# Last 32 tokens routed by pairs of heads, first v loads spread out, and constant inputs of VectorE held in PSUM

## The reference

```python
def block(xt):                                    # peer(): xt are normalised tokens
    qh = (xt @ w_pq).reshape(PEER_BLOCK, PEER_HEADS, 2, half)          # 8 heads x 2 halves
    sub = jnp.einsum('thcd,ckd->thck', qh, sub_keys)                   # 128 scores per half
    top_s, top_i = lax.top_k(sub, PEER_TOPK)                           # 16 best of 128
    cand = (top_s[:, :, 0, :, None] + top_s[:, :, 1, None, :]).reshape(PEER_BLOCK, PEER_HEADS, 256)
    best_s, best_c = lax.top_k(cand, PEER_TOPK)                        # 16 best of 256
    i1 = jnp.take_along_axis(top_i[:, :, 0], best_c // PEER_TOPK, axis=-1)
    i2 = jnp.take_along_axis(top_i[:, :, 1], best_c % PEER_TOPK, axis=-1)
    experts = i1 * PEER_KEYS + i2                                      # one of 128 x 128
    gate = jax.nn.softmax(best_s, axis=-1)
    pre = jnp.einsum('td,thkd->thk', xt, expert_u[experts])
    act = jax.nn.gelu(pre, approximate=False)
    return jnp.einsum('thk,thkd->td', gate * act, expert_v[experts])
```

## Time and profile before

| | us |
|---|---|
| three runs before | 2404.65, 2404.66, 2394.77 (median 2404.65) |
| the profiled execution | 2399.41, span 2397.4 |
| PE busy | 2081.4 (87%) |
| DVE busy | 1669.2 (70%) |
| POOL busy | 1186.3 (49%) |
| ACT busy | 776.1 (32%) |

### The profile page before, as it was taken

The page is one execution under the profiler, slowest core; times in us unless marked ns, Lnnn a source line. Parts: engine busy times, 40 slices in busy tenths (PEclk is TensorE's granted clock), DMA queues, the critical chain, the costliest instruction groups (busy, mean ns, idle before and its releaser), DMA issues.

```text
span 2397.4 us, 34751 instructions
## 1 busy us (share of the span) xinstructions
PE 2081.4 (87%) x12685; PEld 1930.0 (81%) x12685; DVE 1669.2 (70%) x3238; ACT 776.1 (32%) x1230; POOL 1186.3 (49%) x632
## 2 busy tenths in 40 slices
PE   5999998677569898998885888886979999999998
PEld 5989657565449898897784878786879999999998
DVE  2478434443322207699999999994549999999996
ACT  3233233321322324444342333332223333333332
POOL 2326003111003234675674343436888888888884
PEclk9999659895989899999997999998999999999999
DMA  6443255453853114566675666669869989988994
GB/s 223 149 154 112 100 200 216 191 185 103 283 187 132 53 36 154 187 228 208 193 233 173 208 229 244 238 231 336 289 227 324 320 306 318 315 315 308 320 322 143
DMA packets 176598, 520.95 MB, mean 217 GB/s; under 512 B 15153, under 2 KB 86065, under 8 KB 170705
## 3 DMA queue, kind: packets, MB, share of 16 engines
q1 hardware_dynamic: 136560, 290.94, 35.3%
q0 software_dynamic: 36864, 134.23, 17.0%
q10 hardware_dynamic: 3056, 94.24, 9.9%
HBM read 456.81 MB, written 128.49 MB: 244 GB/s over the span
## 4 chain that ended last, share of the span: by engine, by line
DVE 44%; PE 36%; issue 7%; POOL 5%; DMA 3%; ACT 3%; SPq 2%; ACTq 0%; DVEq 0%; PEldq 0%
DVE acc_g L1809 9%; DVE act_l L1793 9%; PE bank L2169 8%; PE bank L2170 7%; PE bank L2171 7%; DVE one L1493 6%; DVE one L1494 5%; DVE rows_g L1662 4%; POOL u_lo L1637 3%; DMA ks<-kc 2%; POOL rows_g L1652 2%; PE bank L438 2%; PE bank L457 1%; DVE eq L1470 1%; PE bank L639 1%
## 5 line engine op out<-in xcount | busy, mean ns | idle before, releaser
L1637 POOL TENSOR_TENSOR u_lo<-u_raw,u_hi 128x1024 fp32r<-128x1024 f32 x128 | 327.8, 2562 | 328.7 <-ACT u_hi L1617 327.7
L2169 PE MATMUL bank<-hn_hi,u_hi 128*128 128x416 f32 x1024 | 381.2, 372 | 67.5 <-POOL u_lo L1637 67.2
L1837 POOL TENSOR_TENSOR v_lo<-v_raw,v_hi 128x1024 fp32r<-128x1024 f32 x128 | 335.4, 2622 | 68.5 <-ACT v_hi L1762 67.3
L2170 PE MATMUL bank<-hn_lo,u_hi 128*128 128x416 f32 x1024 | 368.7, 360 | 0.0
L2171 PE MATMUL bank<-hn_hi,u_lo 128*128 128x416 f32 x1024 | 366.8, 358 | 0.0
L2169 PE MATMUL bank<-a_hi,v_hi 128*128 128x416 f32 x1024 | 360.7, 352 | 1.8 <-DVE a_lo L1799 1.7
L2170 PE MATMUL bank<-a_lo,v_hi 128*128 128x416 f32 x1024 | 358.9, 350 | 0.0
L2171 PE MATMUL bank<-a_hi,v_lo 128*128 128x416 f32 x1024 | 358.8, 350 | 0.0
L1809 DVE SCALAR_TENSOR_TENSOR acc_g<-rows_g,coef,acc_g 128x1024 f32<-128x1024 f32 x127 | 289.2, 2277 | 13.8 <-DMA rows_g<-ev,idx_g 13.3
L2169 PEld LDWEIGHTS bank<-hn_hi,u_hi 128*128 128x128 f32 x1024 | 200.0, 195 | 86.7 <-POOL u_lo L1637 84.1
L1662 DVE CUSTOM_DVE_ANT_0 rows_g<-rows_g,xrep 128x1024 f32<-128x1024 f32 x128 | 187.2, 1466 | 83.0 <-DMA rows_g<-eu_rows,idx_g 82.4
(11 more groups left out here) (360 smaller groups left out, 4358.4 us busy)
## 6 DMA issues: line engine op xcount, KB each, us to landing
u_raw<-eu SPq DMA_DIRECT2D x128, 512.0 KB
v_raw<-ev SPq DMA_DIRECT2D x128, 512.0 KB
k_s<-kc ACTq DMA_DIRECT2D x29, 1104.0 KB
v_s<-vc ACTq DMA_DIRECT2D x29, 1104.0 KB
acts_dram<-act_c SPq DMA_DIRECT2D x128, 208.0 KB
gates_dram<-gst ACTq DMA_DIRECT2D x8, 3328.0 KB, 12.8
gin<-gates_dram SPq DMA_DIRECT2D x32, 832.0 KB
act_l<-acts_dram SPq DMA_DIRECT2D x64, 416.0 KB
```

What stands on the lines that cost most here:

```text
L1637: nc.gpsimd.tensor_tensor(out=u_lo[s][:], in0=u_raw[2 * (x % 2) + s][:], in1=u_hi[s][:].bitcast(F32), op=ALU.subtract).then_inc(dn["ulo"], 1)
L1837: nc.gpsimd.tensor_tensor(out=v_lo[f % 4][:], in0=v_raw[f % 4][:], in1=v_hi[f % 4][:].bitcast(F32), op=ALU.subtract).then_inc(dn["vlo"], 1)
L2169: nc.tensor.matmul(out, ah, bh, start=first and i == 0, stop=False)
L2170: nc.tensor.matmul(out, ah, bl, start=False, stop=False)
```

## The change

Three things. First, part t = 4 (32 tokens) is laid out as four groups of 32 partitions, each with two of the eight heads (`HG` = 4): TensorE writes the scores of head pair g to partitions 32g to 32g + 31, one evacuation replaces four, and every routing step of DVE works on 128 partitions and a quarter of the elements. The turning becomes 12 small matmuls. Second, `load_first` is called at every step of x = 57 to 63 and issues one load at each of its first seven, in place of all eight after x = 50. Third, ACT copies `asc` to PSUM bank 7 and `xrep` to banks 2 and 3 (`twin`) once; DVE's one-hot tiles, the first compare of the lookup and the dots read them there.

```diff
+HG = P // ROUTE[-1][1]
+        x_held, asc_p = twin[:], bank[7][:, 0:P]
@@ sp_ffn
-                if x == LAST_X0:
-                    load_first(sp)
+                    load_first(sp, 2 * (x - FIRST_V + 3) + s)
@@ pe_ffn, half_scores(t)
+                if t == NT - 1:
+                    pe.wait_ge(ff["sub_evac"], 4 * t - 1)
+                    for j in range(4):
+                        for g in range(HG):
+                            last = nc.tensor.matmul(quad(4)[g * w:(g + 1) * w, j, :], qt[:, 4 * g + j, t0:t0 + w], skt_s[:, j % 2, :],
+                                                    start=True, stop=True)
+                    last.then_inc(ff["sub"], 1)
+                    return
@@ pe_ffn, turn_picks(t)
+                if t == NT - 1:
+                    for j in range(3):
+                        for g in range(HG):
+                            last = nc.tensor.matmul(bank[6][g * w:(g + 1) * w, j * P:j * P + w], picks[:, j, 0:PICKS // HG],
+                                                    ident[:, g * w:(g + 1) * w], start=True, stop=True)
@@ act_ffn
             split_u(act, 0, 0, 0)
+            nc.scalar.activation(asc_p, asc, ACT.Copy).then_inc(sx["held"], 1)
+            few_wait(act, "x_in", 32)
+            for b in range(2):
+                nc.scalar.activation(x_held[0:NG, 512 * b:512 * (b + 1)], xrep[0:NG, 512 * b:512 * (b + 1)], ACT.Copy).then_inc(sx["held"], 1)
@@ dve_ffn
-            few_wait(dve, "x_in", 32)
+            few_wait(dve, "held", 3)
             for t, (t0, w) in enumerate(ROUTE):
-                dve.wait_ge(ff["sub_evac"], 4 * (t + 1))
-                top16(t, w, lambda j: tv[0:w, j, :], lambda j: ti[0:w, j, :], lambda j: sub_t[0:w, j, :], 2 * PH)
+                heads = PH
+                if t < NT - 1:
+                    dve.wait_ge(ff["sub_evac"], 4 * (t + 1))
+                else:
+                    dve.wait_ge(ff["sub_evac"], 4 * t + 1)
+                    w, heads = P, PH // HG
+                top16(t, w, lambda j: tv[0:w, j, :], lambda j: ti[0:w, j, :], lambda j: sub_t[0:w, j, :], 2 * heads)
...
-                                  in1=bc(asc[0:w, 0:TOPK], 1, PH * TOPK), op=ALU.is_equal))
-                    chain.link(tt(out=eq[0:w], in0=eq[0:w], in1=bc(tif4[:, :, c, :], 2, TOPK), op=ALU.mult))
+                                  in1=bc(asc_p[0:w, 0:TOPK], 1, heads * TOPK), op=ALU.is_equal))
+                    chain.link(tt(out=eq[0:w, 0:heads], in0=eq[0:w, 0:heads], in1=bc(tif4[:, :, c, :], 2, TOPK), op=ALU.mult))
...
-                    ts(one2[n % HOT][:, j, :], asc, picks_t[:, 1, c:c + 1], None, ALU.is_equal)
-                    last = ts(one1[n % HOT][:, j, :], asc, picks_t[:, 0, c:c + 1], picks_t[:, 2, c:c + 1], ALU.is_equal, ALU.mult)
+                    ts(one2[n % HOT][:, j, :], asc_p, picks_t[:, 1, c:c + 1], None, ALU.is_equal)
+                    last = ts(one1[n % HOT][:, j, :], asc_p, picks_t[:, 0, c:c + 1], picks_t[:, 2, c:c + 1], ALU.is_equal, ALU.mult)
@@ dots
-                nc.vector.tensor_tensor_reduce(out=row, in0=row, in1=xrep[0:NG, :], scale=1.0, scalar=0.0, op0=ALU.mult, op1=ALU.add,
+                nc.vector.tensor_tensor_reduce(out=row, in0=row, in1=x_held[0:NG, :], scale=1.0, scalar=0.0, op0=ALU.mult, op1=ALU.add,
@@ load_first(sp, step)
+            if step == 0:
+                for b in range(2):
+                    sp.wait_ge(gate_out[b], 16 * (GBLOCKS // 2) + 16)
+                load_gates(sp, 0, 0)
+            elif step in (1, 6):
+                load_acts(sp, step // 6, step // 6)
+            elif step in (2, 3):
+                load_v(sp, step - 2, step - 2)
+            elif step == 4:
...
+            elif step == 5:
+                load_gates(sp, 1, 1)
```

More of the change, by code:

```diff
@@ L60 @@
 ROUTE = [(DT, NG)] + [(t0, min(P, DT - t0)) for t0 in range(0, DT, P)]
+HG = P // ROUTE[-1][1]
+assert HG == 4
 ROW_SLOTS, MORE_SLOTS = 3, 5
@@ L1330, in scores_out @@
                     act.wait_ge(ff["sub_free"], t - 1)
+                if t == NT - 1:
+                    act.wait_ge(ff["sub"], 4 * t + 1)
+                    nc.scalar.activation(sub_s[t % 2][:, 0:4, :], quad(4), ACT.Copy).then_inc(ff["sub_evac"], 1)
+                    return
                 for g in range(4):
@@ L1344, in act_ffn @@
                 act.wait_ge(ff["top_exp"], t + 1)
-                nc.scalar.activation(bv[0:w], bv[0:w], ACT.Exp).then_inc(ff["top_expd"], 1)
+                w, heads = (w, PH) if t < NT - 1 else (P, PH // HG)
+                nc.scalar.activation(bv[0:w, 0:heads], bv[0:w, 0:heads], ACT.Exp).then_inc(ff["top_expd"], 1)
             act.sem_inc(ff["gate_bank"], 2)
-            few_wait(act, "x_in", 32)
             with act.Fori(0, GBLOCKS // GB) as i:
@@ L1466, in dve_ffn @@
                 for c in range(2):
-                    chain.link(tt(out=eq3, in0=bc(bhlf[0:w, c].rearrange("p h k -> p (h k)"), 2, TOPK),
-                                  in1=bc(asc[0:w, 0:TOPK], 1, PH * TOPK), op=ALU.is_equal))
-                    chain.link(tt(out=eq[0:w], in0=eq[0:w], in1=bc(tif4[:, :, c, :], 2, TOPK), op=ALU.mult))
+                    chain.link(tt(out=eq3, in0=bc(bhlf[0:w, c, 0:heads].rearrange("p h k -> p (h k)"), 2, TOPK),
+                                  in1=bc(asc_p[0:w, 0:TOPK], 1, heads * TOPK), op=ALU.is_equal))
+                    chain.link(tt(out=eq[0:w, 0:heads], in0=eq[0:w, 0:heads], in1=bc(tif4[:, :, c, :], 2, TOPK), op=ALU.mult))
                     dots(dve, t, 1)
-                    chain.link(nc.vector.tensor_reduce(picks[0:w, c, :], eq3, axis=AX.X, op=ALU.add))
+                    chain.link(nc.vector.tensor_reduce(picks[0:w, c, 0:heads * TOPK], eq3, axis=AX.X, op=ALU.add))
                 dots(dve, t, 1)
                 dve.wait_ge(ff["top_expd"], t + 1)
-                chain.link(nc.vector.tensor_reduce(gsum[0:w, 0, :], bv[0:w], axis=AX.X, op=ALU.add))
-                chain.link(nc.vector.reciprocal(gsum[0:w, 1, :], gsum[0:w, 0, :]))
-                weights = gate_w if t == 0 else picks[:, 2, :]
-                last = tt(out=weights[0:w].rearrange("p (h k) -> p h k", k=TOPK), in0=bv[0:w], in1=bc(gsum[0:w, 1, :], 2, TOPK), op=ALU.mult)
+                chain.link(nc.vector.tensor_reduce(gsum[0:w, 0, 0:heads], bv[0:w, 0:heads], axis=AX.X, op=ALU.add))
+                chain.link(nc.vector.reciprocal(gsum[0:w, 1, 0:heads], gsum[0:w, 0, 0:heads]))
+                weights = gate_w if t == 0 else picks[:, 2, 0:heads * TOPK]
+                last = tt(out=weights[0:w].rearrange("p (h k) -> p h k", k=TOPK), in0=bv[0:w, 0:heads], in1=bc(gsum[0:w, 1, 0:heads], 2, TOPK),
+                          op=ALU.mult)
                 if t:
@@ L1672, in load_gates, with load_first @@
             sp.dma_start(gin[s][:], gates_dram[:, :, bass.ds(4 * k, 4), :].rearrange("b p a t -> p b (a t)")).then_inc(g_in[s], 16)
[L1674 to L1684 removed]
+        def load_first(sp, step):
+            if step == 0:
[7 more added lines that the diff above has]
+            elif step == 4:
+                head = NG - NB * NL
+                sp.dma_start(xg[0:head, :], X[P - head:P, NT - 2, :]).then_inc(sx["xg_in"], 16)
+                sp.dma_start(xg[head:NG, :], X[0:NB * NL, NT - 1, :]).then_inc(sx["xg_in"], 16)
+            elif step == 5:
+                load_gates(sp, 1, 1)
         def sp_dense(sp):
```

44 lines of the change are left out of this document (20 added, 24 removed).

## The result

The changed kernel takes 2326.71 us (median of four runs, 2321.80 to 2331.31), the kernel before in the same comparison 2404.65 (2394.77 to 2409.90). The ratio is 0.968, 95% interval 0.9643 to 0.9717. Run again later it took 2324.92 (five runs), 0.9662 (0.9647 to 0.9677). The profiled execution took 2327.75, its span is 2325.8, its granted clock 0.938 of 2.4 GHz.

The account below looks back on a forecast made before the run. DVE was taken to bound the gate stage and parts t = 2 and 4, PE the dense stage. 2399.4 - 31 (routing) - 18 (gates) - 18 (tail) = 2332, plus 2 gives 2334 us; range about 2312 to 2362.

Parts of the forecast that it names:

- first loads' contention: Tail: first loads meet busy DMA engines, so stores and u tiles come late; 3 us counted against the gain.
- dots and first compare: Routing parts t = 1 to 3: reading PSUM takes 11 us off, bounds 2 and 15.
- part t = 4: Last routing part: head pairs cut DVE's work, PE then sets 52 us against 77; -25, bounds 20 and 31.
- tail: Stretch before the dense stage: first loads one by one and POOL freed by PSUM dots; -18, bounds 0 and -26.
- three terms of routing: Routing: t = 4 -25, dots and compare -11, start copies +5; together -31, bounds -19 and -44.
- signs named beforehand: Profile after: tail 150 to 160 us, no ACT store wait or PE wait there over 5, gates beginning about 1283.
- Gate stage: One-hot tiles from PSUM: 70 us of holds go, 50 of longer steps come; -18, bounds -51 and +29.
- rival in which PSUM inputs are held too: Gate stage: POOL's `u_lo` still holds tiles, stage 362 us (+49), total 2411; chance 0.03.
- rival with a start-up cost of PSUM inputs: Gate stage: each tile costs another 0.065 us, stage 346 us (+33), total 2383; chance 0.05.
- The start copies: Start of routing: ACT's wait for `xrep` and its copies delay PE and ACT; +5 us, bounds 1 and 6.
- the rival in which slack eats half: Fetched rows end t = 4 and the tail's stall returns; -19 - 15 - 3, total 2362; chance 0.16.

Follow-up runs that it names:

- `tiles_sbuf`: Changed kernel with the one-hot tiles and the first compare reading asc in SBUF again: 2345.02 us, ratio 0.9789.
- `lo_twice`: Changed kernel, gate stage's 32 low parts each computed twice: 2322.08 us; second kernel, also with tiles and first compare reading SBUF: 2410.48 us.
- `dots_sbuf`: Changed kernel with the dots reading xrep in SBUF again: 2358.20 us, ratio 0.9819.
- `pairs_alone`: Kernel before with only the last 32 tokens laid out by pairs of heads: 2384.31 us, ratio 0.99.
- `copies_behind`: Changed kernel with ACT's two copies of xrep moved behind the Gelus of the first routing window: 2320.59 us, ratio 0.9655.

## Why the prediction was right, point by point

**The forecast.** 2334 was 7 us above the median, and the faster half of the range holds it. The named mechanisms were seen, except the cost of the first loads' contention, of which nothing shows. The sizes of three terms were off: dots and first compare, part t = 4, and tail. They partly cancelled, so the closeness of the total is in part luck. The terms were off by 14 in sum (-67 against -80.7). The total was off by less, since the forecast added back only 2 of the 5 us between the timed median and the profiled execution before, and since the timed medians differ by 78 and not by 80.7.

The bounds were not put together as the text says. The three terms of routing have bounds that add up to -16 and -45, and in quadrature to about -21 and -39, neither being -19 and -44. The bounds of routing, gates and tail give about 2298 to 2386 in quadrature, not 2312 to 2362, most of it from the gate stage. The measured time lies well inside both. Of the signs named beforehand some were missed narrowly: the tail is 149 us by its cuts, not 150 to 160, and its longest waits are 5.2 us for a store and 5.2 for a low part, not under 5. The gates begin at 1286.3 in a profile that runs 9.1 us late, which is 1277 where 1283 was said.

**Gate stage: -18 forecast, -17.9 measured.** Both its parts are shown separately. The holds are gone, by `tiles_sbuf` (+18.0) and by the two `lo_twice` kernels; the step is 0.06 longer, as worked out from the earlier trace rows. The rival in which PSUM inputs are held too (slower, 2411) would have given `lo_twice` a longer stage, and it stayed at 292.5: the earlier trace rows were read rightly. The section "SBUF: two separate sides" of SBUF — State Buffer in the Trainium skill states the lock; this case adds the price, 2.0 us per subtraction of 2.4. The rival with a start-up cost of PSUM inputs fell with the step: 832 x 0.065, an estimate, would be 54 us more, and the stage is 292.3, not 346. That is the figure of the Trainium skill's VectorE: DVE Perf Modes ("The TRN2 errata"); in a row of instructions that follow each other without a wait it is not to be seen here.

**Dots and first compare, t = 1 to 3: -11 forecast, -24.5 measured. This term was mis-sized.** The parts were 91.7, 82.6 and 85.5 us before and are 89.8, 69.7 and 75.8. I counted how much longer the dots lasted, and let part of it go into the next instruction. In t = 2, where DVE is full, the groups of DVE show where the rest was. Before, 1068.6 to 1151.2:

```profile
L1662 DVE CUSTOM_DVE_ANT_0 rows_g<-rows_g,xrep 128x1024 f32<-128x1024 f32 x13 | 21.8, 1673 | 0.1
...
L1461 DVE CAST bhlf<-bhl 128x256 f32<-128x256 uint32 x1 | 3.2, 3190 | 0.0
L1451 DVE CAST tif<-ti 128x256 f32<-128x256 uint32 x1 | 3.1, 3060 | 0.1
L1478 DVE TENSOR_TENSOR picks<-bv,gsum 128x128 f32<-128x128 f32 x1 | 2.9, 2927 | 0.0
```

After, 1079.5 to 1149.2, the dots and the same two casts:

```profile
L1698 DVE CUSTOM_DVE_ANT_0 rows_g<-rows_g,twin 128x1024 f32<-128x1024 f32 x13 | 15.7, 1209 | 0.1
...
L1485 DVE CAST tif<-ti 128x256 f32<-128x256 uint32 x1 | 0.3, 295 | 0.1
L1495 DVE CAST bhlf<-bhl 128x256 f32<-128x256 uint32 x1 | 0.3, 286 | 0.0
```

6.1 us are the dots. Two casts that the change does not touch last 2.8 and 2.9 less, and the last product of the softmax 2.6 less (0.3 us after). They are 0.3 us instructions that happened to meet a subtraction. Two lookup steps and a copy, +1.5, -0.9 and +0.8, make up the rest of the 12.9. `dots_sbuf` shows that the dots' input decides it: with that one edit undone the same instructions of this stretch are held again, for the same times (1085.5 to 1168.3).

```profile
L1495 DVE CAST bhlf<-bhl 128x256 f32<-128x256 uint32 x1 | 3.1, 3141 | 0.0
L1485 DVE CAST tif<-ti 128x256 f32<-128x256 uint32 x1 | 3.1, 3053 | 0.1
L1512 DVE TENSOR_TENSOR picks<-bv,gsum 128x128 f32<-128x128 f32 x1 | 2.9, 2929 | 0.0
```

The casts have not become free of the hold. In the changed kernel one of t = 3 lasts 2.8 us and one of t = 4 as well. What moved is when POOL subtracts: it used to stand before its gathers until a dot was done, and no longer does. That this shift is what takes the casts of t = 2 out of the subtractions is argued, not tried. Gathers' group on POOL before (985 to 1314):

```profile
L1652 POOL DMA_INDIRECT rows_g<-eu_rows,idx_g x55 | 66.4, 1207 | 61.4 <-DVE pre_g L1662 56.5 <-issue 2.0
```

and after (1000 to 1286):

```profile
L1688 POOL DMA_INDIRECT rows_g<-eu_rows,idx_g x54 | 58.6, 1086 | 10.2 <-issue 3.6 <-DVE pre_g L1698 2.0
```

56.5 us of waiting became 2.0. In `dots_sbuf` it is 37.1 again, with t = 1 to 3 at 92.1, 82.8 and 84.1. So nearly all of it (23.7 us in these parts) belongs to the dots' input. The compare's share is small: routing in `tiles_sbuf` is 366.8, against 359.7 to 363.6 in the four profiles of the changed kernel's routing.

**Part t = 4: -25 forecast, -15.6 measured (75.6 to 60.0). Mis-sized the other way.** I took 52 us from PE's arrival: 48 of products and a last leg of 4. PE's wait before the turning was 4.9, inside the stated 3 to 6. What was too small is the time for PE's work. The sum took PE as ahead of DVE when t = 4 begins, as it was before. Once DVE became faster in t = 1 to 3, PE was not: busy in 261 of the 286 us of the four parts (91%), before in 271 of 329 (82%). The later part starts with PE's debt of the earlier ones. The debt can be counted. These are the instructions that read u's high part between the softmax of t = 3 and that of t = 4, after and then before, 16 matmuls to a product:

```profile
1225.20:1285.20 60.00, 49.14 (x176) 33.64 (x176) 11.45 (x11) 27.15 (x12) 0.97 0.78 254
1236.80:1312.40 75.60, 45.06 (x160) 30.29 (x160) 9.47 (x9) 25.67 (x10) 0.87 0.61 198
```

That is 11 products after and 10 before, and a product is 4.6 us. `pairs_alone` leaves DVE slow in t = 1 to 3; there PE has 10 left, and t = 4 falls by 20.5, to 55.1. In `dots_sbuf` it has 10 as well, and t = 4 takes 54.4. The two terms of routing are one: what DVE gains beyond PE's pace in one part is not gained again in the next. The sum of both, -36 forecast, was -40.1.

**The start copies: +5 forecast, +3.7 at the end of t = 0.** The waits are as estimated (ACT 3.35, copies 1.12 and PE 4.94). But nothing of it can be seen at the end of routing, as `copies_behind` shows. The sign and the size were right at the place, and wrong as a term of the sum.

**Tail: -18 forecast, -26.2 measured.** By the experiments 14.1 are the burst (I had 18 for it, less 3 for contention) and 11.4 the dots (I had 3 of the 8 that POOL's gathers would save). The gathers' 10 us came off nearly in full. POOL's queue was the path for that part: it stood idle in about 29 us of the stage in the changed kernel and in 27 in `dots_sbuf`, so its longer gathers found no slack. The DMA share rose to 0.90 without a cost that can be seen; the rival in which slack eats half, 2362, has no place left.

## What to carry to other kernels

When one engine's instruction holds up another's, count the neighbours too: here the hold also fell on casts of 0.3 us, and on the queue that waited for a dot's result. Two gains that both shorten the same engine's chain are not added until the other engine's work in that stretch has been set against the sum, since the first gain takes away the head start that the second one lived on. A burst of loads on the queue that also carries the pipeline's stores cost 14.1 us here, for 16 us of issues; spread out over steps, the same bytes cost nothing that could be seen, at a DMA share of 0.90.
